# Query norms from turned-back queries, k-q scaled on VectorE, an earlier zeroing and output turn

## The reference, cut to what matters

```python
qkv = silu(causal_short_conv(g_qkv, conv_w))
gq = l2_normalize(gq) * 128 ** -0.5;  gk = l2_normalize(gk)
a_mat = strict(k_beta @ k.T * decay)
sol = triangular_solve(a_mat + I, [v * beta, k_beta * exp(g_cum)])
qk = incl(q @ k.T * decay)
o_gdn = rms_norm(o_gdn, gdn_norm_g) * silu(g_z)
merged = sigmoid(gate_a) * o_gdn + sigmoid(gate_b) * o_att
x = x + merged @ w_out
```

## Time and profile before

| what | us |
|---|---|
| median of 3 runs (lowest, highest) | 936.04 (935.88, 936.29) |
| the profiled execution's own time | 934.9 |
| its span | 933.3 |
| TensorE busy, share of the span | 909.4, 97% |
| VectorE, ScalarE, GpSimd busy | 582.6, 447.9, 120.3 |

### The profile page before, as it was taken

One profiled execution on the slowest core, in us unless ns is written; L12 is line 12 of the kernel. 1 busy time (PEld: TensorE's weight loads), 2 busy tenths in 40 slices (PEclk: granted clock), 3 DMA queues, 4 the chain that ended last, 5 costly groups with the idle time before them and its releaser, 6 DMA issues.

```text
span 933.3 us, 11922 instructions
## 1 busy us (share of the span) xinstructions
PE 909.4 (97%) x4739; PEld 759.6 (81%) x4739; DVE 582.6 (62%) x806; ACT 447.9 (48%) x620; POOL 120.3 (13%) x86
## 2 busy tenths in 40 slices
PE   8999999999999999999999999999999999999998
PEld 5887787888877888888878889888877888888886
DVE  4468988975776566654445747877764655554442
ACT  6265456837353555543335335655554454444431
POOL 0322115848120000000000002100100000000100
PEclk9999999989999999999999999999999999999999
DMA  7774542433234555555658546443550555554561
GB/s 273 188 249 143 180 136 89 134 106 110 74 110 134 169 175 178 182 167 196 196 180 288 186 114 204 137 134 96 176 180 1 180 181 183 188 190 144 180 220 67
DMA packets 83265, 149.73 MB, mean 160 GB/s; under 512 B 8448, under 2 KB 16176, under 8 KB 83088
## 3 DMA queue, kind: packets, MB, share of 16 engines
q1 hardware_dynamic: 80064, 144.55, 47.7%
q10 hardware_dynamic: 2528, 3.63, 1.1%
q0 software_dynamic: 624, 0.87, 0.8%
HBM read 147.59 MB, written 1.44 MB: 160 GB/s over the span
## 4 chain that ended last, share of the span: by engine, by line
PE 84%; DVE 7%; ACT 3%; DMA 3%; issue 1%; POOL 1%; DVEq 0%; SPq 0%; ACTq 0%; POOLq 0%
PE gemm L494 24%; PE gemm L496 23%; PE gemm L495 23%; DMA raw<-in_w_in_dram 2%; PE mixbank L632 2%; PE mixbank L607 2%; DVE w_lo L1648 2%; POOL w_lo L2347 1%; ACT w_hi L1127 1%; PE mixbank L510 1%; PE mixbank L802 1%; PE mixbank L931 1%; PE mixbank L618 1%; DVE mix L1877 1%; DVE mix L1765 1%
## 5 line engine op out<-in xcount | busy, mean ns | idle before, releaser
L1648 DVE TENSOR_TENSOR w_lo<-raw,w_hi 128x2048 fp32r<-128x2048 f32 (+3 forms) x131 | 284.8, 2186 | 179.8 <-ACT w_hi L1127 179.7
L494 PE MATMUL gemm<-w_hi,s_hi 128*128 128x512 f32 (+3 forms) x912 | 354.2, 388 | 8.9 <-DVE w_lo L1648 3.4
L496 PE MATMUL gemm<-w_hi,s_lo 128*128 128x512 f32 (+3 forms) x912 | 346.6, 380 | 0.0
L495 PE MATMUL gemm<-w_lo,s_hi 128*128 128x512 f32 (+3 forms) x912 | 346.0, 379 | 0.0
L1127 ACT ACTIVATE w_hi<-raw 128x2048 fp32r<-128x2048 f32 (+3 forms) x140 | 255.3, 1834 | 173.4 <-DMA raw<-in_w_in_dram 51.6
L494 PEld LDWEIGHTS gemm<-w_hi,s_hi 128*128 128x128 f32 x912 | 172.0, 189 | 43.7 <-issue 7.0
L496 PEld LDWEIGHTS gemm<-w_hi,s_lo 128*128 128x128 f32 x912 | 171.7, 188 | 32.7
L495 PEld LDWEIGHTS gemm<-w_lo,s_hi 128*128 128x128 f32 x912 | 172.1, 189 | 30.9 <-issue 0.5
L2353 POOL TENSOR_TENSOR sm<-sm 128x2 f32<-128x2 f32 (+4 forms) x14 | 27.6, 1972 | 512.1 <-DVE sm L1692 320.6
L2347 POOL TENSOR_TENSOR w_lo<-raw,w_hi 128x2048 fp32r<-128x2048 f32 x9 | 41.4, 4607 | 162.3 <-ACT w_hi L1127 162.3
L494 PE MATMUL gemm<-w_hi,hT_hi 128*128 128x512 f32 x128 | 50.6, 395 | 0.0
(11 more groups left out here) (311 smaller groups left out, 910.0 us busy)
## 6 DMA issues: line engine op xcount, KB each, us to landing
raw<-in_w_in_dram SPq DMA_DIRECT2D x40, 1024.0 KB, 5.1
raw<-in_w_mlp_up_dram SPq DMA_DIRECT2D x16, 1024.0 KB, 5.6
raw<-in_w_mlp_down_dram SPq DMA_DIRECT2D x16, 1024.0 KB, 5.1
raw<-in_w_gate_dram SPq DMA_DIRECT2D x10, 1024.0 KB, 5.1
raw<-in_w_up_dram SPq DMA_DIRECT2D x10, 1024.0 KB, 5.1
raw<-in_w_down_dram SPq DMA_DIRECT2D x10, 1024.0 KB, 5.0
raw<-in_w_out_dram SPq DMA_DIRECT2D x8, 1024.0 KB, 5.1
raw<-in_w_xkv_dram SPq DMA_DIRECT2D x8, 1024.0 KB, 5.1
```

The costliest lines, as they stand in the source:

```text
L494: nc.tensor.matmul(o, hi, wh, start=kt == 0, stop=False)
L495: nc.tensor.matmul(o, hi, wl, start=False, stop=False)
L496: last = nc.tensor.matmul(o, lo, wh, start=False, stop=kt == blk["kt"] - 1)
L1648: V.tensor_tensor(w_lo[:, s, 0:kn, 0:width], raw[:, s, 0:kn, 0:width], w_hi[:, s, 0:kn, 0:width].bitcast(F32), ALU.subtract)\
```

## The change

- The queries' squares no longer go through `Y2` and the ones column. `queries_back` turns two heads of `YT` at a time into the banks `G[0]`, two groups behind the first level and two behind the second. ScalarE squares them there and sums along the row (activation with `accum_out`), straight into `SSK`. GpSimd adds the small constant and takes the power, and signals `gdn_qr`.
- `query_rows` is now one VectorE step for each head that scales by the key's root and multiplies by the decay; ScalarE's scaling and GpSimd's masking of `QK` are gone.
- `key_query` runs in four banks, the first three right among fills 10 to 12. The four `turned_back` of the values follow in a row, each in a bank of its own.
- ScalarE zeroes `XT` and copies the values ahead of the first z gate. The two stores to `base_x` and the placements have semaphores of their own (`base_kept`, `base_turn_kept`; `base_back`, `base_turned`).
- The output's first half is turned before the last quarter of gate a. VectorE's splits of the output weights stand after the first half. The output block runs as two quarters, turn, two quarters, where it was one and three.

The engines' edits, with lines of no interest left out:

```diff
-ROOTS = ("mix", "att", "gdnq", "o0", "o1", "mlp", "mix2", "fox", "mem", "ret", "xk", "xattn", "xq", "ffn")
+ROOTS = ("mix", "att", "o0", "o1", "mlp", "mix2", "fox", "mem", "ret", "xk", "xattn", "xq", "ffn")
...
-Y2 = view(ar, 10416, 4, 2, SEQ)
...
-KQ_BANK = (0, 1, 2, 0)
+KQ_BANK = (0, 1, 2, 3)
+QUERIES = G[(B_GA + 1) % 2]
...
-        sp.wait_ge(sem("base_kept"), 32)
+        sp.wait_ge(sem("base_kept"), 16)
...
+        bank = M[3 if i < 4 else KQ_BANK[i - 4]]
...
-                last = nc.tensor.transpose(M[3][:, (2 * j + t) * P:(2 * j + t + 1) * P], YT[:, 2 * e + j, P * t:P * t + P], ident)
+                last = nc.tensor.transpose(bank[:, (2 * j + t) * P:(2 * j + t + 1) * P], YT[:, 2 * e + j, P * t:P * t + P], ident)
...
+    def queries_back(p):
...
+        if p < 2:
+            pe.wait_ge(sem(f"ev{p}"), B_Z + 2)
+        else:
+            pe.wait_ge(sem("gdn_q2"), p - 1)
+        for j in range(2):
+            for t in range(NT):
+                last = nc.tensor.transpose(QUERIES[p % 2][:, (2 * j + t) * P:(2 * j + t + 1) * P], YT[:, 2 * p + j, P * t:P * t + P], ident)
+        last.then_inc(sem("gdn_qs"), 1)
...
-    def query_sums():
...
-        pe.wait_ge(sem("gdn_q2"), 4)
-        pe.wait_ge(sem("gdn_at"), 4)
-        for p in range(4):
-            for j in range(2):
-                for t in range(NT):
-                    c = 8 * t + 2 * p + j
-                    last = nc.tensor.matmul(M[3][:, c:c + 1], Y2[:, p, j, P * t:P * t + P], cst[:, C_ONES:C_ONES + 1], start=True, stop=True)
-        last.then_inc(sem("gdn_qs"), 1)
...
     key_key(3)
-    fill(11)
-    query_sums()
     pe.wait_ge(sem("gdn_y"), 10)
     key_query(0)
+    fill(11)
     pe.wait_ge(sem("gdn_y"), 11)
     key_query(1)
-    fill(12)
-    pe.wait_ge(sem("root_asked"), root("gdnq"))
-    turned_back(4)
     pe.wait_ge(sem("gdn_y"), 12)
     key_query(2)
-    pe.wait_ge(sem("gdn_kqc"), 1)
+    pe.wait_ge(sem("gdn_at"), 4)
     key_query(3)
-    fill(13)
-    pe.wait_ge(sem("back_act"), 5)
-    turned_back(5)
-    fill(14)
-    pe.wait_ge(sem("back_act"), 6)
-    turned_back(6)
-    fill(15)
-    pe.wait_ge(sem("back_act"), 7)
-    turned_back(7)
+    fill(12)
+    for i in range(4):
+        pe.wait_ge(sem("gdn_qk"), i + 1)
+        turned_back(4 + i)
+    for n in range(13, 16):
+        fill(n)
...
-        pe.wait_ge(sem("gdn_kqc"), 4)
...
-        pe.wait_ge(sem("base_back"), 16 * NB)
+        pe.wait_ge(sem("base_turned"), 8 * NB)
...
+        pe.wait_ge(sem("base_back"), 8 * NB)
...
+    for p in range(2):
+        queries_back(p)
     mm(B_GA, quarters=[1])
...
+    for p in range(2, 4):
+        queries_back(p)
     mm(B_GA, quarters=[2])
...
-    mm(B_GA + 1)
+    pe.wait_ge(sem("gdn_q2"), 4)
+    mm(B_GA + 1, quarters=range(3))
...
-        mm(B_O, turned=8, quarters=range(1) if half == 0 else range(1, 4))
+        if half == 0:
+            mm(B_GA + 1, quarters=[3])
+        mm(B_O, turned=8, quarters=range(2 * half, 2 * half + 2))
...
-        act.wait_ge(sem("gdn_y"), 5 + p)
-        nc.scalar.activation(Y2[:, p], YT[:, 2 * p:2 * p + 2, :], ACT.Square).then_inc(sem("gdn_q2"), 1)
...
+        act.wait_ge(sem("gdn_qs"), p + 1)
+        if p >= 2:
...
+            act.wait_ge(sem("gdn_q2"), p - 1)
+        for j in range(2):
+            for t in range(NT):
+                n = 2 * j + t
+                c = 8 * t + 2 * p + j
+                ins = nc.scalar.activation(junk[:, P * (4 * (p % 2) + n):][:, 0:P], QUERIES[p % 2][:, P * n:P * n + P], ACT.Square, scale=0.5, accum_out=SSK[:, c:c + 1])
+        ins.then_inc(sem("gdn_q2"), 1)
...
-        nc.scalar.activation(dst, M[3].rearrange("p (j t d) -> p j t d", j=2, t=2), ACT.Copy).then_inc(sem("back_act"), 1)
+        nc.scalar.activation(dst, M[KQ_BANK[i]].rearrange("p (j t d) -> p j t d", j=2, t=2), ACT.Copy).then_inc(sem("back_act"), 1)
...
-    def query_rows(u):
...
-        act.wait_ge(sem("gdn_kq"), u + 1)
-        for q in range(4):
-            n = 4 * u + q
-            ins = nc.scalar.activation(QK[:, n, :], M[KQ_BANK[u]][:, P * q:P * q + P], ACT.Copy, scale=RQK[:, 16 + n:17 + n])
-        ins.then_inc(sem("gdn_kqc"), 1)
...
-            sig(gate(b, ZG[:, t, cols], t, HRS[:, t:t + 1], [("gdn_qs", 1)]), "z_tanh")
+            sig(gate(b, ZG[:, t, cols], t, HRS[:, t:t + 1]), "z_tanh")
...
-    query_squares(0)
...
-    query_squares(1)
...
-    query_squares(2)
...
-    query_squares(3)
...
-    act.wait_ge(sem("gdn_kdf"), 1)
-    query_rows(0)
-    query_rows(1)
+    act.wait_ge(sem("gdn_kq"), 4)
+    nc.scalar.activation(XT, spread(cst[:, C_ZERO:C_ZERO + P], 1, 16), ACT.Copy).then_inc(sem("base_zero"), 1)
     split(B_GA, 0)
+    for i in range(4):
+        values(i)
     gate_z(B_Z)
-    values(0)
-    query_rows(2)
-    query_rows(3)
-    nc.scalar.activation(XT, spread(cst[:, C_ZERO:C_ZERO + P], 1, 16), ACT.Copy).then_inc(sem("base_zero"), 1)
-    values(1)
...
-    act.dma_start(base_x[1].rearrange("m n j i -> (m n) j i"), BXT).then_inc(sem("base_kept"), 16)
+    act.dma_start(base_x[1].rearrange("m n j i -> (m n) j i"), BXT).then_inc(sem("base_turn_kept"), 16)
     split(B_GA, 1)
-    values(2)
-    act.wait_ge(sem("base_kept"), 32)
+    act.wait_ge(sem("base_turn_kept"), 16)
...
-        place_base(act, 1, m, XI).then_inc(sem("base_back"), 16)
-    values(3)
+        place_base(act, 1, m, XI).then_inc(sem("base_turned"), 16)
...
             split(B_GA + 1, k)
+            query_squares(2 * k)
+            query_squares(2 * k + 1)
...
+    act.wait_ge(sem("o_sq"), 2)
+    turn_hi(banks=range(2))
     for t in range(NT):
         gate(B_GA + 1, TMP[:, t], t, HRS[:, t:t + 1], [("gate_used", 1)]).then_inc(sem(f"ev{t}"), 1)
-    act.wait_ge(sem("o_sq"), 2)
-    turn_hi()
+    turn_hi(banks=range(2, 4))
...
+    def query_rows(u):
...
+        dve.wait_ge(sem("gdn_dm"), u + 1)
+        dve.wait_ge(sem("gdn_kq"), u + 1)
+        for q in range(4):
+            n = 4 * u + q
+            ins = V.scalar_tensor_tensor(QK[:, n, :], M[KQ_BANK[u]][:, P * q:P * q + P], RQK[:, 16 + n:17 + n], DM[:, n, :], ALU.mult, ALU.mult)
+        ins.then_inc(sem("gdn_qk"), 1)
...
-    dve.wait_ge(sem("gdn_qs"), 1)
-    V.tensor_scalar(SSK[:, 0:16], M[3][:, 0:16], 0.25, EPS, ALU.mult, ALU.add).then_inc(sem("root_asked"), 1)
+    for u in range(4):
+        query_rows(u)
...
-    dve.wait_ge(sem("root"), root("gdnq"))
+    dve.wait_ge(sem("gdn_qr"), 1)
     output_norm(1)
-    split(B_O, 0)
     times_z(1)
     output_factors(1)
...
     sig(V.scalar_tensor_tensor(o, oa[:, :, cols], 0.5, o, ALU.mult, ALU.add), "o_done")
+    split(B_O, 0)
+    turn_lo(banks=range(2))
+    split(B_O, 1)
...
-        if t == 0:
-            turn_lo(banks=range(2))
...
-    split(B_O, 1)
...
-    for u0 in (0, 2):
-        for u in (u0, u0 + 1):
-            n = slice(4 * u, 4 * u + 4)
-            pool.wait_ge(sem("gdn_kqc"), u + 1)
-            pool.tensor_tensor(QK[:, n, :], QK[:, n, :], DM[:, n, :], ALU.mult).then_inc(sem("gdn_qk"), 1)
-        for u in (u0, u0 + 1):
...
-            pool.wait_ge(sem("back_pe"), 5 + u)
-            n = slice(4 * u, 4 * u + 4)
-            parts = [blocks_of(v, BASE_LEVEL, 1) for v in (LT[:, n, :], AT[:, n, :], spread(cst[:, C_LEV:C_LEV + P], 1, 4))]
-            pool.tensor_tensor(*parts, ALU.mult).then_inc(sem("inv_lt"), 1)
+    for u in range(4):
...
+        pool.wait_ge(sem("back_pe"), 5 + u)
+        n = slice(4 * u, 4 * u + 4)
+        parts = [blocks_of(v, BASE_LEVEL, 1) for v in (LT[:, n, :], AT[:, n, :], spread(cst[:, C_LEV:C_LEV + P], 1, 4))]
+        pool.tensor_tensor(*parts, ALU.mult).then_inc(sem("inv_lt"), 1)
...
-    power("gdnq", RQK[:, 0:16], SSK[:, 0:16], 16)
+    pool.wait_ge(sem("gdn_q2"), 4)
+    pool.tensor_tensor(SSK[:, 0:16], SSK[:, 0:16], EPSC.to_broadcast([P, 16]), ALU.add).then_inc(sem("pool_step"), 1)
+    pool.wait_ge(sem("pool_step"), 8)
+    pool.tensor_tensor(RQK[:, 0:16], SSK[:, 0:16], MHALF[:, 0:16], ALU.pow).then_inc(sem("gdn_qr"), 1)
```

## The result

The changed kernel takes **928.25 us** (median of 4 runs, 927.78 to 929.99), the kernel before beside it 936.16 us (4 runs, 935.88 to 936.39): a ratio of 0.9924, 95% interval 0.9909 to 0.9939, or 7.9 us less. The forecast was 927.8. The two profiled executions are 934.9 and 928.26 us, 6.6 apart; the other 1.3 us is the distance of the execution profiled before from its own median.

A forecast was written before the change was run, and what follows sets the result against it. TensorE, busy 97% of a 933.3 us span, was taken as the bound. Conv stage 7.5, transposes -1.8 and output 2.5 summed to 8.2 us, taken from the median 936.04 to give 927.8, range 926.0 to 931.0.

The forecast's parts named there:

- Conv stage: Up to the inverse's first level: sums, idle time and low clock go, so level four starts 7.5 us sooner.
- The new waits: TensorE in the conv stage: 0.2 us ahead of key_query(2), 0.7 ahead of gate a's first quarter, 0.1 for XI.
- the solve starts 0.3 us sooner: VectorE's solve in the conv stage: blocks land 2.0 us after issue, at 206.1, so it starts before the old 206.47.
- GpSimd's masks: Ahead of the first level: 0.72 us each, starting at 213.6, wanted from 219.8, hidden by the quarter of gate a.
- with no cover the first would cost 0.7: First level: the first GpSimd mask would cost 0.7 us if gate a's quarter did not hide it.
- k-q to VectorE and the zeroing: Conv stage: with ScalarE's query rows gone and other work earlier, XI's store leaves at 213.6 instead of 218.28.
- Queries turned back: Between the inverse's levels: 16 added TensorE transposes lose 1.8 us; ScalarE's squares end before its level copies are wanted.
- The output: From the end of L906 through out's first block: the new order gains 2.5 us, bounds 1.5 and 3.5.
- the 28.5 us: Old order's time from L906's end through out's first block, two waits and low clock included; new order forecast at 26.0.
- The first, a fall of the clock elsewhere: Rival: the clock falls at the output's new 1.7 us wait and turn, costing about 1.8 us: 929.6; chance 0.18.
- The second: Rival: late placements through DRAM or late query_rows delay level four onward by 1 to 3 us: 930.0; chance 0.14.
- The third: Rival: TensorE's saved time returns as waits for VectorE at gate a's first quarter, nothing gained: 935.5; chance 0.04.

The follow-up runs named there:

- e10: The kernel before with query_sums taken out and queries_back with ScalarE's squares put in, all else in its old place: 939.87 us, ratio 1.0048.
- e11: e10 with GpSimd's four LT masks moved ahead of the four QK products: 929.13 us, ratio 0.9934 against the kernel before.
- e3: The changed kernel with k-q products scaled on ScalarE and masked on GpSimd again, behind the LT masks: 928.00 us, ratio 0.9914.
- e2: The changed kernel with ScalarE's zeroing of XT put back behind the values and first z gate: 928.12 us, ratio 0.9916.
- e1: The changed kernel with the output part alone put back in the old order: 928.39 us (5 runs), ratio 0.9930.
- e8: The changed kernel with the output's second half turned mid second quarter of out, VectorE's second out split behind that half: 926.83 us, ratio 0.9915.
- e12: The kernel before with 32 equal columns per sum and key products moved into the idle time ahead of query_sums: 934.49 us, ratio 0.9979.
- e5: The kernel before with key_query(0) ahead of fill 11 and key_query(1) ahead of query_sums, one-column products kept: 933.47 us, ratio 0.9981.
- e4: The kernel before with query_sums writing 32 equal columns for each sum in place of one: 934.94 us, ratio 1.0.
- e13: The changed kernel unedited, run again on the same chip as a further output variant: 927.72 us, ratio 0.9917.

## Why the prediction was right, and where its steps were off

The forecast gain was 8.2 us and the medians give 7.9, but the stages of the two traces give 7.15. That the total came out within 0.3 us is in part luck: 0.75 us of it lies outside the stages worked out and was not located. The prediction's bounds of 926.0 to 929.3 do not follow from its terms, either; their bounds added up give 926.3 to 930.5, still inside the range.

**Conv stage: right.** Forecast 7.5 us up to the first level, measured 7.05. The 8.4 us taken away are sums, idle time and clock as they were read. The new waits: 0.32 ahead of `key_query(2)` for the forecast 0.2; 0.87 ahead of gate a's quarter for 0.7; none for XI, for 0.1. `query_rows` took 4.22 us for the 4.2 put there. The step that was a little off is "the solve starts 0.3 us sooner": its blocks landed 2.2 us after issue, not 2.0, and it started 0.1 sooner.

**GpSimd's masks: right, by luck more than by reason.** The prediction let them start right behind the solve, since the k-q products ahead of them were gone, and put "with no cover the first would cost 0.7". They did start there, at 214.80. But each took 1.69 us beside VectorE's splits, not 0.72, and the prediction did not ask what late masks would cost: with two products left ahead of them it is 10.7 us, e10 against e11. The two waits that arise are 2.9 us; the clock is the rest. So no term of the sum for this edit was needed in the forecast, and yet the whole gain stands on it. Taking the sums out alone makes this kernel slower.

**k-q to VectorE and the zeroing: right about the fit, wrong about what they bring.** The prediction had the store of XI leave 4.7 us earlier because ScalarE was relieved. It leaves at 214.75 for 218.28, which is 4.3 us earlier without the offset, but e3 and e2, which take back the one or the other, cost nothing: with either, the store leaves at 215.37 or 215.11, as soon as the solve is over.

**Queries turned back: right.** 1.8 us forecast, 1.7 measured. ScalarE's squares ended at 230.9 and 237.6, ahead of its copies at 232.51 and 239.00, and the only wait in the levels is the 0.33 that was there before.

**The output: the term that was mis-sized.** Forecast 2.5, measured 1.8. The waits came as worked out, 1.83 for 1.6 and 1.07 for 0.8, and the power took 2.54 us for 2.8. But the 28.5 us that the new order was held against had the stretch at 1.2 GHz in it. e1 shows the old order at full clock only 0.25 us behind the new one: the term was the clock's, and at an equal clock the reorder is worth next to nothing. As a term for certain it was wrong, since two of e1's five runs have the lower clock.

**The rivals.** The first, a fall of the clock elsewhere for about 1.8 us, fits the one run of 929.99 us with a mean clock of 0.998; that it is the cause is argued from e1's and e8's runs, not seen in a trace. Its price of 1.8 us is that of one short stretch: in e10 a fall that lasted from 223 to 240 us cost 7.5. The second did not happen: placements landed 2.5 us after issue at most. The third's mechanism, VectorE pacing gate a, is real but cost 0.87 us and not six. The fourth's waits stayed away. A rival that ends slower did exist, and I had not named it: TensorE early at work whose masks are late. It was one edit away.

## What to carry to other kernels

Before taking work off the bounding engine, list what the others must have done by its new, earlier arrival: here two masks behind two products turned 6.5 us gained (e11) into 4.7 lost (e10). A short wait among small products costs more than its length when the clock falls behind it, so first set the order of such helpers. And of a time read in a stretch at 1.2 GHz say which part is clock before it is credited to a new order.

## What the runs showed of the hardware

- The clock fell with shorter waits than the 1.6 to 2.0 us that the prediction had read: 1.03 us ahead of sixteen records of 64 columns (e10), 1.01 us among the same products (e12), and with no wait at all ahead of one-column products (e5). In e10 the granted clock stayed at 0.50 through 230 to 240 us although TensorE was busy for all of it. The output's waits of 2.0 and 1.0 us had the fall before and none in e10 and e11: from the last products to the next stage's turn it is 41.45, 39.87 and 39.93 us.
- The same kernel falls in some executions and not in others: mean clocks of 1.0 and 0.998 are about 2 us apart (e1, e8). Whether waits or narrow products bring it on stays open; e4, e5 and e12 gave one profile each.
- One VectorE step of 0.2 us took 4.51 us because GpSimd had started first. GpSimd's operations stretch in the same way: k-q products 1.24 to 3.3 us, masks 0.70 to 1.69, an eight-column power 1.64 to 3.61.
- Executions of one kernel differ already ahead of the change, at two waits for weights' low parts. The first, near 50 us, took 1.44 us before and 1.82 after, but 0.92 when the changed kernel was profiled again (e13); the second, near 113 us, took 1.00, 1.23 and 0.97. Over all 14 traces the second key-key group starts between 187.02 and 188.87 us.
